# A two-layer decoder step: fewer picks inside the samples' scan, block rows on GpSimd, and an earlier release of the expert gathers

## The reference, cut to what matters

```python
# the scan of the mixer, for each of 8 groups of 4 heads, over one chunk
cum   = cumsum(dt * a);  decay = exp(cum_t - cum_s), causal
y     = ((C B^T) * decay) @ xdt + (C @ h) * exp(cum)
h_new = h * exp(cum_last) + B^T @ (tail * xdt)        # h: one state per sample sequence
# PEER, for each token and each of 8 heads
s     = q . sub_keys                # two halves of 128 scores
top16 of each half -> 16 x 16 grid of sums -> top16 -> 16 of 16384 experts, gate = softmax
out   = sum over 128 picks of gate * gelu(x . expert_u[i]) * expert_v[i]
```

## Time and profile before

| | |
|---|---|
| median of three runs | 2444.46 us |
| the profiled execution, its span | 2444.89 us, 2443.1 us |
| busy: PE, DVE, ACT, POOL | 1741.4, 1569.0, 260.7, 1340.1 us |
| moved by DMA | 859.09 MB, mean 352 GB/s |
| chain that ended last | POOL 23%, DMA 18%, PE 11%, issue 9%, DVE 8% of the span |
| mean granted TensorE clock | 0.830 |

### The profile page before, as it was taken

The page is one execution under the profiler, slowest core; times in us unless marked ns, Lnnn a source line. Parts: engine busy times, 40 slices in busy tenths (PEclk is TensorE's granted clock), DMA queues, the critical chain, the costliest instruction groups (busy, mean ns, idle before and its releaser), DMA issues.

```text
span 2443.1 us, 22858 instructions
## 1 busy us (share of the span) xinstructions
PE 1741.4 (71%) x7437; PEld 762.4 (31%) x7437; DVE 1569.0 (64%) x3812; ACT 260.7 (11%) x628; POOL 1340.1 (55%) x1496
## 2 busy tenths in 40 slices
PE   7999799494406666678788676886756767556678
PEld 4577658334400010022335223451213412001112
DVE  2388777999798757652644898878765644733321
ACT  2133212001000000011110111110011100000000
POOL 0011653266547777755665556665645664677774
PEclk9999899596756666689889887787877978699999
DMA  4332257399979999999999999999999999999997
GB/s 162 111 131 70 94 181 257 119 407 417 417 268 407 420 420 419 420 409 416 416 419 416 413 415 364 419 416 417 416 414 420 408 415 386 396 419 420 419 419 294
DMA packets 270247, 859.09 MB, mean 352 GB/s; under 512 B 26288, under 2 KB 31344, under 8 KB 270128
## 3 DMA queue, kind: packets, MB, share of 16 engines
q0 software_dynamic: 184320, 671.17, 67.9%
q1 hardware_dynamic: 85808, 186.46, 20.3%
HBM read 845.26 MB, written 12.17 MB: 351 GB/s over the span
## 4 chain that ended last, share of the span: by engine, by line
POOL 23%; DMA 18%; PE 11%; issue 9%; DVE 8%; ACT 0%; SPq 0%; POOLq 0%; DVEq 0%; ACTq 0%
POOL arena L2491 23%; DMA arena<-peer_v,arena 11%; PE banks L880 4%; DVE arena L2137 3%; PE banks L1072 3%; DMA wring<-w_q 2%; DMA arena<-peer_u,arena 2%; DMA wring<-ple_w_gate 1%; DMA wring<-peer_w_query 1%; PE banks L820 1%; DMA wring<-w_o 1%; PE banks L989 1%; DVE arena L1951 1%; PE banks L558 1%; DVE arena L1948 1%
## 5 line engine op out<-in xcount | busy, mean ns | idle before, releaser
L2137 DVE SCALAR_TENSOR_TENSOR arena<-arena,banks 128x1024 f32<-128x1024 f32 x640 | 763.1, 1219 | 451.5 <-DMA arena<-peer_u,arena 445.1
L1072 PE MATMUL banks<-arena 128*32 128x512 f32 x2560 | 703.5, 726 | 383.3 <-DMA arena<-peer_v,arena 376.9
L2491 POOL DMA_INDIRECT arena<-peer_u,arena x640 | 606.2, 947 | 386.2 <-issue 186.4
L2491 POOL DMA_INDIRECT arena<-peer_v,arena x640 | 607.4, 949 | 351.1 <-issue 173.4
L1072 PEld LDWEIGHTS banks<-arena 128*32 128x32 f32 x2560 | 93.7, 117 | 870.3 <-DMA arena<-peer_v,arena 704.9
L880 PE MATMUL banks<-wring,uT 128*128 128x512 f32 (+3 forms) x448 | 217.5, 634 | 40.7 <-DMA wring<-w_q 17.8
L558 PE MATMUL banks<-cst,arena 128*128 128x128 f32 (+2 forms) x349 | 61.3, 330 | 147.3 <-DVE arena L2153 82.2
L634 PE MATMUL banks<-uT,wring 128*128 128x320 f32 x512 | 139.1, 433 | 0.0
L880 PEld LDWEIGHTS banks<-wring,uT 128*128 128x128 f32 (+1 forms) x448 | 78.0, 184 | 188.2 <-issue 153.5
L2424 POOL COPY arena<-arena 128x3 f32<-128x3 f32 x32 | 6.0, 188 | 207.5 <-ACT arena L1416 207.5
L634 PEld LDWEIGHTS banks<-uT,wring 128*128 128x128 f32 x512 | 96.7, 190 | 39.8 <-issue 0.4
(11 more groups left out here) (270 smaller groups left out, 1883.2 us busy)
## 6 DMA issues: line engine op xcount, KB each, us to landing
wring<-peer_w_query SPq DMA_DIRECT2D x40, 1024.0 KB, 18.4
wring<-ssm_w_in SPq DMA_DIRECT2D x24, 1024.0 KB, 7.2
wring<-w_q SPq DMA_DIRECT2D x18, 1024.0 KB, 20.4
wring<-ssm_w_out SPq DMA_DIRECT2D x16, 1024.0 KB, 9.1
wring<-ple_w_gate SPq DMA_DIRECT2D x12, 1024.0 KB, 12.2
arena<-peer_u,arena POOLq DMA_INDIRECT x640, 11.6
arena<-peer_v,arena POOLq DMA_INDIRECT x640, 9.9
out_sample_ssm<-arena SPq DMA_DIRECT2D x16, 512.0 KB, 3.8
```

What stands on the lines that cost most here:

```text
L1072: mm = pe.matmul(sums(t, at, half), place_of(t, at), rows_buf[:, k, half * 512:(half + 1) * 512], start=at < spots(t), stop=False, skip_gr ...
L2137: dve.scalar_tensor_tensor(rows_buf[:, k, :], rows_buf[:, k, :], 1.0, u_now, ALU.mult, ALU.mult, accum_out=pact[:, n % 2, at:at + 1]).then ...
L2491: pool.indirect_dma_start(rows_buf[:, k, :], None, tables[kind], bass.IndirectOffsetOnAxis(ap=rows, axis=0))\
```

## The change

Three things are changed. VectorE takes 2, 2, 1, 0, 0 steps of picking in the turns of groups 3 to 7, so one quad instead of two and two fifths; fifteen steps are left for phase 0, and `first_select` of PE and ScalarE counts fifteen before its own part. GpSimd makes the block rows, in the group's own turn, ahead of `ctm`; its wait for the exponentials' bank (`ec`, whose input lay in the same area) moves ahead of them, and PE waits for GpSimd's. And `scan_over` is told behind the last new states, ahead of the scaling and the transposed rows; GpSimd waits for the last group's square on ScalarE too, as that still reads `yt`, before the gathers.

```diff
@@ -650,7 +650,7 @@
                                        h0[(2 * g + b // 4) % 4][:, b % 4, 128 * i:128 * i + 128],
                                        start=(b == 0), stop=(b == 7))
                 mm.then_inc(*full(("inter", 2, g)))
-                pe.wait_ge(*dve_done.at(("bm", g)))
+                pe.wait_ge(*pool_done.at(("bm", g)))
                 acc = {(q, c): claim(pe, ("hupd", 2 * g + q, c)) for q in range(2) for c in range(2)}
                 for b in range(2):
                     for q in range(2):
@@ -1128,7 +1128,7 @@
             second_select = select(0, 1)
 
             def first_select():
-                for _ in range(8):
+                for _ in range(15):
                     yield
                 yield from finish_select(0, 0)
 
@@ -2000,16 +2000,7 @@
                     add_to_h("out", 0, 0, 1)
                     norm("ffn0", FFN_SLOT, (0,))
                 if g >= 3:
-                    advance(early_picks, (3, 3, 2, 2, 2)[g - 3])
-
-            def block_rows(g):
-
-                if g >= 2:
-                    dve.wait_ge(*full_at(("hupd", 2 * g - 3, 1)))
-                elif g == 0:
-                    dve.wait_ge(*full_at("ec"))
-                s(dve.tensor_tensor(bm[:, g % 2, :, :], repeat(btok[:, 2, g * 128:(g + 1) * 128], 4),
-                                    spread(cst[:, C_SEQ:C_SEQ + 4], 128), ALU.mult), dve_done, ("bm", g))
+                    advance(early_picks, (2, 2, 1, 0, 0)[g - 3])
 
             def new_states(g):
 
@@ -2034,10 +2025,6 @@
                     decays(n + 2)
                 if n + 1 < 3 * GROUPS:
                     mix(n + 1)
-                if n == 2 * GROUPS - 1:
-                    block_rows(0)
-                if t == 2 and g + 1 < GROUPS:
-                    block_rows(g + 1)
                 y = yt[0:R, x, :]
                 if n == 2 * GROUPS:
                     add_to_h("out", 0, 0, 0)
@@ -2067,6 +2054,8 @@
                 s(dve.tensor_tensor(zz, zz, y, ALU.mult), dve_done, ("gated", t, g))
                 if t == 2:
                     new_states(g)
+                    if g == GROUPS - 1:
+                        tell("scan_over")
                 if t == 0:
                     bank = filled(dve, ("state", t, g))
                     freeing(dve.tensor_copy(hT[:, g, :], bank[:, 0:256]), ("state", t, g))
@@ -2081,7 +2070,6 @@
                 if t == 2:
                     after_sample_turn(g)
             turn_rows(2)
-            tell("scan_over")
 
             def take_indices(l, t):
 
@@ -2454,12 +2442,14 @@
                 s(pool.tensor_tensor(heads(dxs[0:R, x, :]), xg, spread(d_bc[0:R, 4 * g:4 * g + 4], 64), ALU.mult),
                   pool_done, ("dxs", t, g))
                 if t == 2:
+                    pool.wait_ge(*freed("ec"))
+                    s(pool.tensor_tensor(bm[:, g % 2, :, :], repeat(btok[:, 2, g * 128:(g + 1) * 128], 4),
+                                         spread(cst[:, C_SEQ:C_SEQ + 4], 128), ALU.mult), pool_done, ("bm", g))
                     if g >= 2:
                         pool.wait_ge(*full_at(("inter", 2, g - 2)))
                     c = ctm[:, g % 2, :, :]
                     diag = bass.AP(c.tensor, c.offset, [list(c.ap[0]), [72, 8], [1, 8]])
                     s(pool.tensor_copy(diag, bcT[:, 8 + g, 256:320].rearrange("p (b w) -> p b w", b=8)), pool_done, ("ctm", g))
-                    pool.wait_ge(*freed("ec"))
                     for q in range(2):
                         blk = 2 * g + q
                         pool.wait_ge(*h0_in[blk % 4].at(blk))
@@ -2475,6 +2465,7 @@
             for blk in (14, 15):
                 pool.wait_ge(*hnew_out[blk % 2].at(blk))
             pool.wait_ge(*dve_done.at("scan_over"))
+            pool.wait_ge(*act_done.at(("gsq", 2, GROUPS - 1)))
             for ph in range(7):
                 for kind, n, at in phase_blocks(ph):
                     (l, t), (k, use) = UNITS[n], turn_of[kind, n, at]
```

## The result

The changed kernel takes **2464.18 us** (median of 5 runs, 2461.05 to 2470.26), the kernel before 2444.46 in the same session: ratio 1.0085, 95% interval 1.0072 to 1.0097. So it is slower, by 19.7 us where 10 were forecast; the time lies inside the range, near its upper end. The profiled execution took 2464.18 us.

The account below looks back on a forecast made before the run. VectorE's work and waits from 407.6 to the copy of tile 1's u at 726.3 were taken as the bound. Late product 2.1 us later, picks +20.5, hidden waits -15.0, score +2.4: 10 us later, 2454.5 us, range 2435 to 2467.

Parts of the forecast that it names:

- The scan: Samples' scan behind the third group: 64.8 us shrinks to 47.8 with picks and block rows gone; first dot 24 us earlier.
- The release: Gathers released behind the last states: GpSimd's first gather at 460 instead of 485.6, rows in time for the first dot.
- The hold: First gather phase: PE waits for the fourth score's copy, behind the second quad; VectorE stands 27.5 us for the late output product.
- The picks that come back: Seven picking steps leave the scan for the first gather phase and add 20.5 us of VectorE work there.
- The cover: VectorE's 15.0 us of waits for gathered rows, between 600 and 660 us, hide that much of the returning picks.
- 2.4 was added for a score: Tile 1's first late score, ready some 666 us, while VectorE reaches it at 664: 2.4 us added.
- the way through the late add: Sum from VectorE taking the late output product 2.1 us later: 2.1 + 20.5 - 15.0 = 7.6, plus 2.4: 10 us later.
- the forecast's own list of side steps: First gather phase: 36 side steps behind dots 4, 8, 11, 15, 18, 22 and so on; second quad takes the first five.
- the rival that kept the 15 us: The rival "More lost", in its part where row waits stay at 15 us because weights and gathers still meet; chance 0.16.
- PE not held: Rival: the fourth score's bank is free when PE asks, so the 27.5 us go; about -11 us, 2434; chance 0.21.
- More lost: Rival: states' round trip limits the last groups, or row waits stay at 15 us; 2462 to 2470; chance 0.16.
- No change: Rival: scan closes in 43 rather than 48 us and the score isn't waited for; +3.2 us, 2448; chance 0.21.

Follow-up runs that it names:

- the rows back on VectorE: Changed kernel with only the block rows moved back from GpSimd to VectorE: 2464.34 us, 1.0091 of the kernel before.
- the fourth score apart: Changed kernel with tile 0's fourth score given rows of its own, so its copy doesn't wait for the second quad: 2440.28 us, 0.9982 of the kernel before.
- the old split: Changed kernel with twelve picking steps in the scan again, leaving only GpSimd's block rows and the earlier release: 2441.71 us, 0.9986 of the kernel before.
- halved weights: Changed kernel with each late query's weight load bringing half its bytes (late scores not the reference's): 2462.65 us, 1.0069 of the kernel before.
- the old release: Changed kernel with gathers released behind the last transposes of the tile's rows, as before: 2465.96 us, 1.0079 of the kernel before.

## Why the prediction was right and where it was wrong

*What bounds the kernel: right.* The copy of tile 1's u carries the end; behind it every profile takes 1717 us, give or take 3. The block rows ahead of 407.6 gave nothing that shows, as said: the 4.7 us by which the changed profile is ahead at its first pick are there with the rows back on VectorE too (403.46).

*The scan: right.* 47.8 us forecast from the first picks to its end, 49.5 measured (402.99 to 452.5); first dot 23.8 us earlier forecast, 22.4 and 22.9 measured from the first pick on. *The release* came as forecast (460 forecast, 456.2 measured, 460.9 on the clock of the kernel before), and is worth nothing at the copy.

*The hold: right in cause and size, its clock by luck.* The stand took 27.4 us (27.5 forecast), and the fourth score apart shows its cause: PE starts right behind that copy, wherever the copy stands. That PE began at 503.5, forecast 503.6, is luck: this profile runs 4.7 us early, and from the first pick on it is 100.5 us against 96.0 forecast. Of these 4.5 us, 1.4 lie ahead of the first dot and 2.9 are first rows that came late (dots 2 and 3), which the forecast had at nothing.

*The picks that come back:* 20.5 forecast, 19.7 by VectorE's busy time (235.4 against 215.7 us).

*The cover: wrong, and this is the failed step.* "What hides them is the 15.0 us of waiting for rows, since those picks now fall among the dots that had waited" let all of it go, and 2.4 was added for a score. Between the first dot and the copy the waits fell from 16.3 to 12.0 us, 4.3 instead of 15; where 15.0 stood, 9.1 are left. The score wasn't waited for. From the first dot's shift on the four measured terms close: -22.4 + 19.7 + 27.4 - 4.3 = +20.4, with 20.8 in the profile. With the forecast's terms the sum is -23.8 + 20.5 + 27.5 - 15.0 + 2.4 = 11.6 (10.0 by the way through the late add). The cover's 10.7 us are more than the whole difference of 8.8.

I had subtracted work from waits as if they lay in one place. Counted in the traces, the picks of this tile stand behind dots 4 to 29 before and 4 to 54 after; the seven that came stand behind dots 32 to 54, which the forecast's own list of side steps gives when it is carried on. The waits of the kernel before are at dots 74 to 96 (72 to 94 in my text), at the end of a stretch of bare dots that begins at 44. First and last late row behind 530 us before:

```profile
613.39 1.22 DVE L2137 SCALAR_TENSOR_TENSOR arena<-arena,banks 128x1024 f32<-128x1024 f32 x1 [0.54 <-DMA arena<-peer_u,arena]
...
655.10 1.22 DVE L2137 SCALAR_TENSOR_TENSOR arena<-arena,banks 128x1024 f32<-128x1024 f32 x1 [0.51 <-DMA arena<-peer_u,arena]
```

The last moved pick and the first late row behind 530 us after:

```profile
612.21 0.19 DVE L1993 TENSOR_TENSOR arena<-arena 128x32 f32<-128x32 f32 x1
...
646.04 1.22 DVE L2125 SCALAR_TENSOR_TENSOR arena<-arena,banks 128x1024 f32<-128x1024 f32 x1 [0.15 <-DMA arena<-peer_u,arena]
```

What the picks gave was a later start of the bare stretch (dot 62) and a shorter one: 15 late rows instead of 21. This has nothing to do with the hold: between the old split and the fourth score apart, two kernels without it, the waits fall by 6.1 us (16.8 to 10.7) while VectorE's busy time grows by 19.0. And VectorE's 27 us stand could not serve as cover either: the gathers stop when fourteen slots are full. My text named that, as a reason to expect less than all of it, and then entered all of it in the sum; the rival that kept the 15 us had the better idea, at 0.16: 9.1 us stayed where it said 15 and I none.

*Rivals.* PE not held, 2434: PE was held; without the hold it is 2440. More lost, 2462 to 2470: it came out there, by the waits for rows and not by the states' round trip. No change, 2448, asked for a scan of 43 us; it took 49.5.

What stays open: how the full DMA engines divide between gathers and loads. Bare dots go 1.9 us apart where weights are loaded, whichever these are, and not nearer to the 1.24 of GpSimd's issues; the runs show it, halved weights did not change it, and no run holds the loads back or takes them away. And whether the moved picks, the hold mended, are worth anything by themselves: 0.9982 with them, 0.9986 without.

## What to carry to other kernels

Work hides a wait where it stands between the instructions that wait; put ahead of them, some 20 us of it hid 4 to 6 us here. What waited here were rows gathered beside weight loads, so the place to fill was where the loads run. Before subtracting a stage's idle time from added work, list by index where the work lands and where the waits are. And when steps of one engine are moved later, look up who reuses the buffers that they free: here a score copy two engines away, a bank and a whole product hung on the one half of a tile.

## What the hardware showed

Row gathers and weight loads together filled the DMA engines at 416 GB/s (share 1.03), and rows came 1.9 us apart there, against one issue of GpSimd every 1.24 us:

```profile
664.09 1.22 DVE L2125 SCALAR_TENSOR_TENSOR arena<-arena,banks 128x1024 f32<-128x1024 f32 x1 [0.70 <-DMA arena<-peer_u,arena]
666.02 1.22 DVE L2125 SCALAR_TENSOR_TENSOR arena<-arena,banks 128x1024 f32<-128x1024 f32 x1 [0.71 <-DMA arena<-peer_u,arena]
667.94 1.22 DVE L2125 SCALAR_TENSOR_TENSOR arena<-arena,banks 128x1024 f32<-128x1024 f32 x1 [0.69 <-DMA arena<-peer_u,arena]
```

GpSimd's pace, where no slot held it:

```profile
460.65 0.94 POOL L2482 DMA_INDIRECT arena<-peer_u,arena  x1 [0.30 <-issue]
461.89 0.94 POOL L2482 DMA_INDIRECT arena<-peer_u,arena  x1 [0.30 <-issue]
```

This is the changed kernel. What the DMA engines did in the 25 us from 646 to 671, the gathers' queue and then the loads' (packets, MB, share of 16 engines):

```profile
q0 software_dynamic: 2078, 7.57, 74.2%
q1 hardware_dynamic: 1411, 2.79, 28.8%
```

A gather brings 128x1024 f32 (0.52 MB), so 7.57 MB are 14.4 gathers, one in 1.7 us on average (an estimate from this row): beside the loads, that was the rows' share of the full engines. With half the query weights the spacing was 1.94 us, beside the loads that follow them.

GpSimd's first gather took 2.4 to 2.9 us in all eleven profiles in which it follows a wait for a store (the early release), and 1.14 or 1.15 in the three with the old release. Why is not tested.
